# Turning the merge blocks of the gated delta rule with 64x64 products instead of 128x128 transposes

## The reference

```python
def gated_delta_chunked(q, k, v, beta, g):
    c = DN_CHUNK
    ...
    k_beta = k * beta[..., None]
    a_kk = jnp.where(strict, jnp.einsum("bhnid,bhnjd->bhnij", k_beta, k) * decay, 0.0)
    eye = jnp.eye(c, dtype=q.dtype)
    t_inv = lax.linalg.triangular_solve(eye + a_kk, jnp.broadcast_to(eye, a_kk.shape),
                                        left_side=True, lower=True, unit_diagonal=True)
    u = jnp.einsum("bhnij,bhnjd->bhnid", t_inv, v * beta[..., None])
    w = jnp.einsum("bhnij,bhnjd->bhnid", t_inv, k_beta * jnp.exp(gcum)[..., None])
    ...

def bidir_gated_deltanet(q, k, v, beta, g):
    fwd = gated_delta_chunked(q, k, v, beta[:, :, 0], g[:, :, 0])
    flip = lambda t: jnp.flip(t, axis=1)
    bwd = flip(gated_delta_chunked(flip(q), flip(k), flip(v), flip(beta[:, :, 1]), flip(g[:, :, 1])))
    return fwd + bwd
```

## Time and profile before

| what | value |
|---|---|
| median of 3 runs | 3696.68 us |
| the three runs | 3694.2, 3716.29 and 3696.68 us |
| the profiled execution's own time | 3705.52 us |
| its span, first to last instruction | 3703.7 us |
| mean granted TensorE clock | 0.979 of full |

### The profile page before, as it was taken

The page is one execution under the profiler, slowest core; times in us unless marked ns, Lnnn a source line. Parts: engine busy times, 40 slices in busy tenths (PEclk is TensorE's granted clock), DMA queues, the critical chain, the costliest instruction groups (busy, mean ns, idle before and its releaser), DMA issues.

```text
span 3703.7 us, 49734 instructions
## 1 busy us (share of the span) xinstructions
PE 3574.8 (97%) x18732; PEld 2859.8 (77%) x18732; DVE 1674.7 (45%) x2646; ACT 986.4 (27%) x1742; POOL 1810.1 (49%) x1057
## 2 busy tenths in 40 slices
PE   7999899999999989999999899999999999999999
PEld 5767677878776767787888788888887789888887
DVE  5255645727435574572741263345344124344342
ACT  3235532201223463220111233232011124232010
POOL 5532336656652232665666433536656422536654
PEclk9999899999999999999999999999999999999999
DMA  3220113222332102332323211223223423212222
GB/s 117 91 72 32 34 60 97 97 85 92 96 114 69 46 2 69 102 97 84 95 88 96 85 47 57 75 63 94 97 91 102 103 86 97 74 57 91 97 91 91
DMA packets 84152, 299.18 MB, mean 81 GB/s; under 512 B 8600, under 2 KB 9752, under 8 KB 83608
## 3 DMA queue, kind: packets, MB, share of 16 engines
q1 hardware_dynamic: 81904, 290.11, 24.3%
q10 hardware_dynamic: 1032, 2.62, 0.6%
q0 software_dynamic: 1056, 4.19, 0.4%
HBM read 285.88 MB, written 11.01 MB: 80 GB/s over the span
## 4 chain that ended last, share of the span: by engine, by line
PE 80%; DVE 10%; ACT 4%; issue 4%; DMA 1%; DVEq 0%; POOL 0%; ACTq 0%; SPq 0%; POOLq 0%
PE PSUM L346 19%; PE PSUM L347 19%; PE PSUM L345 19%; PE PSUM L906 2%; PE PSUM L1939 1%; PE PSUM L907 1%; PE PSUM L908 1%; PE PSUM L1943 1%; DVE PSUM L504 1%; DVE SLABS L1567 1%; DVE OUTER_PRODUCT L1564 1%; PE PSUM L961 1%; PE PSUM L1503 1%; DVE ACT_HI L1830 1%; PE PSUM L918 1%
## 5 line engine op out<-in xcount | busy, mean ns | idle before, releaser
L296 POOL TENSOR_TENSOR W_LOS<-SLABS,W_HI 128x1024 fp32r<-128x1024 f32 (+3 forms) x454 | 1139.8, 2511 | 37.9
L294 POOL TENSOR_SCALAR W_HI<-SLABS 128x1024 fp32r<-128x1024 f32 (+3 forms) x454 | 501.6, 1105 | 1289.6 <-DMA SLABS<-w_k 1289.6
L346 PE MATMUL PSUM<-H_LO,W_HI 128*128 128x512 f32 x2480 | 981.7, 396 | 0.0
L345 PE MATMUL PSUM<-H_HI,W_HI 128*128 128x512 f32 x2224 | 884.5, 398 | 26.0 <-DVE H_LO L489 20.9
L347 PE MATMUL PSUM<-H_HI,W_LOS 128*128 128x512 f32 x2224 | 885.1, 398 | 0.0
L346 PEld LDWEIGHTS PSUM<-H_LO,W_HI 128*128 128x128 f32 x2480 | 467.3, 188 | 118.6 <-issue 2.7
L345 PEld LDWEIGHTS PSUM<-H_HI,W_HI 128*128 128x128 f32 x2224 | 419.4, 189 | 132.1 <-issue 22.2
L347 PEld LDWEIGHTS PSUM<-H_HI,W_LOS 128*128 128x128 f32 x2224 | 418.8, 188 | 97.9
L504 DVE TENSOR_TENSOR PSUM<-PSUM,FACTORS 128x512 f32<-128x512 f32 x282 | 195.4, 695 | 560.2 <-PE PSUM L347 495.9
L345 PE MATMUL PSUM<-ACT_HI,W_HI 128*128 128x512 f32 x928 | 369.7, 398 | 9.8 <-DVE ACT_LO L1832 8.1
L347 PE MATMUL PSUM<-ACT_HI,W_LOS 128*128 128x512 f32 x928 | 372.1, 401 | 0.0
(11 more groups left out here) (503 smaller groups left out, 4970.3 us busy)
## 6 DMA issues: line engine op xcount, KB each, us to landing
SLABS<-w_k SPq DMA_DIRECT2D x406, 512.0 KB, 3.5
SLABS<-w_k SPq DMA_DIRECT2D x32, 768.0 KB, 4.3
SLABS<-w_k SPq DMA_DIRECT2D x32, 640.0 KB, 3.9
X<-xT SPq DMA_DIRECT2D x2, 2048.0 KB, 9.9
X<-w_k SPq DMA_DIRECT2D x2, 2048.0 KB, 9.2
SLABS<-w_k SPq DMA_DIRECT2D x16, 256.0 KB, 3.0
ARENA<-gate_rows SPq DMA_DIRECT2D x8, 512.0 KB, 5.4
bias_rows<-SQ ACTq DMA_DIRECT2D x1, 2560.0 KB
```

The costliest lines, as they stand in the source:

```text
L294: nc.gpsimd.tensor_scalar(hi, raw, 1.0, 0.0, MUL, ADD).then_inc(pool_step, 1)
L296: nc.gpsimd.tensor_tensor(lo, raw, hi.bitcast(F), SUB).then_inc(slab_split[s], 1)
L345: mm(out, w_hi, rhs[0](k), start=k == first, stop=False)
L346: mm(out, w_hi, rhs[1](k), start=False, stop=False)
```

## The change

Line 1462 issued a transpose of the full 128x128 matrix against the 128x128 identity. It now issues an ordinary product of the 64x64 block at h0 with the 64x64 block of the identity at the same place, into the 64x64 block of PSUM that ScalarE reads. The data are 32-bit floats as before. The waits, the semaphore, the order and the reader are the same.

```diff
                         pe.wait_ge(*nth("t32", u + 1))
                         for k in range(8):
-                            last = nc.tensor.transpose(tl(pair2(b + 1), k), tl(mat(q, d), k), C("ident"))
+                            block = slice(h0, h0 + 64)
+                            last = mm(tl(pair2(b + 1), k)[block, block], tl(mat(q, d), k)[block, block], C("ident")[block, block],
+                                      start=True, stop=True)
                         last.then_inc(dn["turn_psum"], 1)
```

## The result

The changed kernel is slower. Its median is 3748.36 us (4 runs, 3742.28 to 3750.71) against 3695.44 us for the kernel before beside it, a ratio of 1.0118 with a 95% interval from 1.0093 to 1.0144. The forecast was 3697 us, within 1%, with a range up to 3711 us. It was wrong.

A forecast was written before the change was run, and what follows sets the result against it. TensorE, busy 97% of the span, was taken to bound the kernel, mostly with the large products of lines 345 to 347. The path's +0.3 us on the profiled 3705.52 us, carried to the median of 3696.68, gave 3697 us, range 3688 to 3711.

The forecast's parts named there:

- the most at stake: Direction 1's transposes, the only ones on the path: 11.03 us in all, 0.3% of the time.
- Removed and added: Direction 1, per layer: transposes of 3.27 and 1.73 us replaced by two-instruction 64x64 products of 3.5 and 1.94 us.
- the sum: Direction 1's groups on the path, gaps included: +0.03 and +0.11 us a layer, +0.3 us for two layers.
- (b): Rival: 64x64 products at half clock cost 1.94 us as at full, or clock rises sooner; -2.8 us, chance 0.11.
- (c): Rival: each new product is one 61 ns instruction, so the path gains 6.1 us in all; chance 0.06.
- Beside the path: Direction 0's 64 transposes, covered by VectorE and ScalarE waits: slowing them was to cost nothing.
- The 0.3 us: Direction 0's expected lengthening from the new form: 0.15 us a group, two groups.
- The 1.38 us of cover: ScalarE's idle time before line 1290, waiting for VectorE, which was to hide any delay of direction 0.
- rival (a): Clock follows width of work in the merges; without transposes it rises later: +11.7 us, 3708.4 us, chance 0.28.
- worst case for the merges: The clock rival's extreme: lines 1358, 1469 and 1475 at half clock throughout, about 35 us.

The follow-up runs named there:

- e5: Changed kernel with ten wide products of zeros (128x128 by 512 columns) ahead of line 1454 in direction 1's first group: 3727.67 us, ratio 1.0060.
- e13: Changed kernel with twelve wide products of zeros in one piece ahead of the turning step (line 1463) of each group: 3710.27 us, ratio 1.0012.
- e11: Changed kernel with wide products of zeros ahead of line 1454 in every group (14 and 18 in first groups, 4 in second): 3734.37 us, ratio 1.0080.
- e7: Kernel before, transposes kept, with 18 wide products of zeros ahead of line 1454 in direction 1's first group: 3701.75 us, ratio 0.9990.

## Why the prediction was wrong

*What bounds the kernel, and the most at stake.* The transposes on the path are 11 us, and I concluded that nothing the edit does to their own cost can gain more. That stands. It said nothing about what they do for other lines.

*Removed and added.* Right. Two instructions a product; 32 loads in 3.49 us at half clock for 3.5 forecast, and in 1.94 us at full clock (e5, layer two) for 1.94; a gap of 0.12 us before line 1358 for 0.06. At an equal clock direction 1 differs by 0.2 us a layer (20.49 against 20.28), where the sum had 0.14. The mechanisms (b) and (c) are out.

*Beside the path.* "Direction 0 costs nothing" failed. The 0.3 us counted on the level rising at 408.1 us as before, and it did not. The 1.38 us of cover existed, but 64-wide and 32-wide steps at half clock used it up and made the direction late by another 4.9 us a layer.

*The sum and rival (a).* This is the step that failed. The sum on the path, +0.3 us, priced the edited step and its gaps and left every other line at the clock it had before. The lines behind the step lost their clock: of the 10.9 us that each direction 1 took longer the forecast had 0.14. Rival (a) named that mechanism, and its place (still at half when the next 64-wide step begins), and I gave it 0.28. Its size was off too: I priced one more spell of 3.4 us in a group, the shortest that the rows showed, and came to 11.7 us. The level stayed down for 89 and 79 us, and the stretches lost 42.4 us. My worst case for the merges, about 35 us if the level does not rise in two full groups, is what came: 31.5 us. Two things were left out. First, I took it for evidence against (a) that lines 1469 and 1475 held the full level by themselves. Holding a level and bringing it back are different, and in the runs even the holding is not sure: in e5 the same series held it in one layer and lost it in the other. Second, I priced only the merges. The recurrence behind them lost 7.7 and 3.2 us, because it started at half clock and needed nearly 22 us in the first layer and 12 in the second to get out.

The Trainium skill ("TensorE: Matmul & The Clock Gate", Part 4) says that transposes do not count as activity for the clock. I had set the trace against it, rightly: in the runs with transposes in a single group of direction 1 the level came back 0.4 us (the last group, at 460.8 us) and 1.4 us (the first, at 443.3 us) behind their end, and with none not before the recurrence. I should have drawn the conclusion: if the transposes were what raised the clock, the edit that shrinks them must name what raises it instead.

*The numbers.* With (a) at its true size, 43 us for 11.7, the kernel lands at 3740 us, beyond the 1% line. The medians are further apart, 52.9 us; the two profiled executions differ by 43.1 us, and the one of the kernel before lay 8.8 us above its median. The chance of 0.02 for slower hung on that one price.

## What to carry to other kernels

Before an edit makes matmuls smaller, look at the granted clock ahead of them and behind them: if the level rises while they run, they pay for what follows. Cutting full-width work in a stretch of narrow work can cost more than it saves, and the loss shows in lines that the edit does not touch. If the full-width work has to go, put some in one piece right ahead of the narrow steps, as in e13, which lost at most 0.3%. In the idle time further ahead it gave back only about half of the loss (e5) or a third (e11). Check the clock of the next stages rather than the duration of the piece.

## What the runs showed that I had not expected

- TensorE was busy almost without a gap with 32-wide and 64-wide products and stayed at half clock (0.50 in direction 1 of the changed kernel, 32.28 us busy of 33.18). Weights of 64 rows by 128 columns did no better (0.50, 38.71 of 39.60).
- The place of the same 96 products changed the time by 77 us.
- The scatter of the kernel before goes with the clock. Its runs beside e5 went from 3688.01 us at a mean clock of 0.985 to 3716.42 us at 0.975. In which stretches they lost it is not on record.
- Transposes do not bring the level back every time. In the kernel before with 18 wide products (e7), direction 0 was 31.20 us long at a clock of 0.84 in one layer and 35.75 at 0.67 in the other. In the second, the sixteen transposes of its first group left the level at half, and it came back only at 1365.5 us, behind those of the second group. The transposes, and a stretch behind them:

```profile
1346.39 3.65 PE L1465 MATMUL PSUM<-CONST,ARENA 128*128 128x128 f32 x16
...
1350.00:1360.00 10.00, 9.99 (x183) 0.50 0.01 2
```

- From line 586 of layer two to the end, which no edit touches, the profiled executions took either 2237 to 2242 us (with the last group's transposes 3709.2 - 1469.9 = 2239.3) or 2249 to 2257 us (the kernel before 3703.7 - 1453.6 = 2250.1). The cause is open. The stretches at half clock in it add up to 47 to 61 us in the shorter ones and 61 to 81 us in the longer, but e11 (2242.2 us) and e7 (2250.3 us) are 8 us apart with nearly the same sum. Differences of 10 us between single executions are not to be read as an edit's.
- What exactly the clock needs to come back stays open. The runs say what mostly brought it back (16 full-width transposes or products in a row, ten to eighteen wide products in a row) and what mostly did not (narrow work, or pairs of wide products between series of 64x64 ones). The failures of the first kind, in e7 and at the start of the recurrence, are not explained.
